# Second expert stage: two more leading weight places used once; the table of slots and the gate row fetched by ScalarE's queue

## What is computed

```python
tokens = modulate(x, norm_ffn[l], sh2, sc2)            # layer 0: context and latent, 512 tokens; layer 1: latent, 256
f = hier_moe(tokens, w_group[l], b_group[l], w_expert[l], b_expert[l], w1[l], w3[l], w2[l])
x = x + gt2 * f                                        # gt2: the gate row, 1024 numbers, one row for all tokens
```

## Time and profile before

| | |
|---|---|
| median of 3 runs | 2339.06 us (2337.82 to 2340.0) |
| the profiled execution | 2338.98 us |
| its span in the trace | 2337.2 us |
| busy: PE, DVE, ACT, POOL | 2186.6, 976.9, 347.4, 168.1 us |
| moved by DMA | 603.00 MB, mean 258 GB/s |
| granted clock of TensorE | 0.992 |
| stage 0, first to last `up` | begins at 367 us |
| stage 1, first `up` to last `add_pair` | 1112.6 to 1573.3 us |

### The profile page before, as it was taken

One profiled execution on the slowest core, in us unless ns is written; L12 is line 12 of the kernel. 1 busy time (PEld: TensorE's weight loads), 2 busy tenths in 40 slices (PEclk: granted clock), 3 DMA queues, 4 the chain that ended last, 5 costly groups with the idle time before them and its releaser, 6 DMA issues.

```text
span 2337.2 us, 25791 instructions
## 1 busy us (share of the span) xinstructions
PE 2186.6 (94%) x9558; PEld 1099.7 (47%) x9558; DVE 976.9 (42%) x1821; ACT 347.4 (15%) x943; POOL 168.1 (7%) x206
## 2 busy tenths in 40 slices
PE   5989999999999999989999888899899999999998
PEld 2436554333333344455333333335668744567843
DVE  3567433444433357573222222234721345561245
ACT  2006211000000010061000000001520001341100
POOL 1210002000000002230100000000000000000000
PEclk9999999999999999999999999999999999999999
DMA  9674557999999952244999999994324444514442
GB/s 374 248 278 154 198 181 302 420 420 421 422 421 421 421 224 72 75 169 162 364 420 420 420 421 421 421 382 126 109 72 158 153 167 134 180 37 136 152 145 98
DMA packets 150764, 603.00 MB, mean 258 GB/s; under 512 B 12660, under 2 KB 25716, under 8 KB 101136
## 3 DMA queue, kind: packets, MB, share of 16 engines
q1 hardware_dynamic: 145264, 595.26, 65.2%
q0 software_dynamic: 4736, 5.99, 0.7%
q10 hardware_dynamic: 672, 0.49, 0.1%
HBM read 606.89 MB, written 4.72 MB: 262 GB/s over the span
## 4 chain that ended last, share of the span: by engine, by line
PE 71%; DMA 12%; DVE 11%; ACT 2%; POOL 2%; issue 2%; SPq 1%; DVEq 0%; ACTq 0%; POOLq 0%
PE psum L2810 15%; DMA extra<-in_w 11%; PE psum L3024 10%; PE psum L3046 8%; PE psum L2327 7%; PE psum L2851 7%; PE psum L2820 6%; PE psum L2241 4%; PE psum L2905 4%; PE psum L2469 2%; PE psum L2340 2%; POOL rstd L500 1%; PE psum L2549 1%; DVE arena L1840 1%; PE psum L2588 1%
## 5 line engine op out<-in xcount | busy, mean ns | idle before, releaser
L1753 DVE TENSOR_TENSOR X<-X,psum 128x512 f32<-128x512 f32 x192 | 132.1, 688 | 269.4 <-PE psum L2820 268.4
L2810 PE MATMUL psum<-ring,arena 128*64 128x512 f32 x608 | 220.7, 594 | 12.6 <-DMA ring<-in_w 12.6
L3024 PE MATMUL psum<-hT,ring 128*128 128x256 f32 x1024 | 222.9, 381 | 2.6 <-DVE hT L1872 2.6
L2810 PE MATMUL psum<-arena 128*64 128x512 f32 x512 | 221.9, 595 | 0.7 <-ACT arena L968 0.7
L3024 PEld LDWEIGHTS psum<-hT,ring 128*128 128x128 f32 x1024 | 195.5, 191 | 29.7 <-DVE hT L1872 3.0
L2820 PE MATMUL psum<-arena 128*128 128x512 f32 x384 | 178.3, 601 | 0.0
L2327 PE MATMUL psum<-ring,hT 128*128 128x512 f32 x384 | 167.9, 593 | 1.9 <-DVE hT L1528 0.7
L2851 PE MATMUL psum<-ring,arena 128*64 128x512 f32 x408 | 167.3, 594 | 0.9 <-DVE arena L1844 0.9
L2241 PE MATMUL psum<-con,arena 128*128 128x128 f32 (+1 forms) x848 | 120.7, 282 | 33.0 <-DVE arena L1840 10.5
L2851 PE MATMUL psum<-extra,arena 128*64 128x512 f32 x328 | 146.4, 596 | 0.0
L2241 PEld LDWEIGHTS psum<-con,arena 128*128 128x128 f32 (+1 forms) x848 | 93.9, 142 | 88.2 <-issue 25.5
(11 more groups left out here) (396 smaller groups left out, 3073.8 us busy)
## 6 DMA issues: line engine op xcount, KB each, us to landing
ring<-in_w SPq DMA_DIRECT2D x127, 1024.0 KB, 21.9
arena<-in_w SPq DMA_DIRECT2D x72, 1024.0 KB, 18.8
ring<-in_w_ff SPq DMA_DIRECT2D x64, 1024.0 KB, 5.8
extra<-in_w SPq DMA_DIRECT2D x62, 1024.0 KB, 20.0
rows<-in_w SPq DMA_DIRECT2D x61, 1024.0 KB, 19.7
ring<-in_w_mod SPq DMA_DIRECT2D x32, 1024.0 KB, 13.5
gate<-in_w SPq DMA_DIRECT2D x29, 1024.0 KB, 23.0
hT<-in_w SPq DMA_DIRECT2D x18, 1024.0 KB, 16.5
```

The costliest lines, as they stand in the source:

```text
L1753: dve.tensor_tensor(x, x, bank, ALU.add).then_inc(v_free, 1)
L2810: inst = pe.matmul(out[64 * e:64 * e + 64, :], xgT[:, b, k, 64 * e:64 * e + 64], m, start=k == 0, stop=k == KB - 1)
L3024: inst = pe.matmul(bank[:, SEQ * f:SEQ * f + SEQ], w[k][:, at:at + P], hT[:, k, 0:SEQ], start=k == 0, stop=k == KB - 1)
```

## The change

1. Stage 1 has two more leading places, 9 (all of it) and 22 (new: `arena` 12288 to 14336). They are second and third in the order of use, so 20 chunks lead. They are used once; after them the old 18 places go round. SP issues place 9 behind place 7 and place 22 behind place 15, both with the same waits as these.
2. `pick_first`, `pick_second` and the scratch of the squares in stage 1 move to `arena` 8192 to 10240.
3. In both stages ACT, not SP, waits for `x_scattered` and fetches the table; it does so ahead of its first silu. SP goes from the leading chunks straight to the next chunk.
4. The gate row of stage 1 is fetched by ACT, when the first four chunks are used, ahead of the first silu. DVE's wait for it moves behind `slot_shares` of pair 0, ahead of line 1851.

```diff
-STEADY_PLACES = [[LEAD_PLACES[n][i % len(LEAD_PLACES[n])] for i in range(12 * LEAD_PAIRS[n])][-12:] for n in range(2)]
+ONCE = [9, 22]
+LEAD_ISSUE = [LEAD_PLACES[0], [12, 20, 21, 4, 5, 7, 9, 14, 17, 19, 18, 15, 22, 0, 6, 1, 2, 3, 8, 16]]
+LEAD_PLACES[1][1:1] = ONCE
+def lead_sequence(n):
+    places = list(LEAD_PLACES[n])
+    again = [p for p in places if p not in ONCE]
+    while len(places) < 12 * LEAD_PAIRS[n]:
+        places += again
+    return places[:12 * LEAD_PAIRS[n]]
+LEAD_SEQUENCE = [lead_sequence(n) for n in range(2)]
+STEADY_PLACES = [x[-12:] for x in LEAD_SEQUENCE]
...
-        pick_first = arena[:, 13312:13824].rearrange("p (t n) -> p t n", t=4)
+        pick_first = arena[:, 9216:9728].rearrange("p (t n) -> p t n", t=4)
...
-        pick_second = arena[:, 12800:13312].rearrange("p (t n) -> p t n", t=4)
+        pick_second = arena[:, 9728:10240].rearrange("p (t n) -> p t n", t=4)
...
-            at = {15: 10240, 16: 15360, 17: 6144, 18: 2048, 19: 4096}[i]
+            at = {15: 10240, 16: 15360, 17: 6144, 18: 2048, 19: 4096, 22: 12288}[i]
...
-                    squares([2, 3], arena[:, 12288:14336].rearrange("p (t n) -> p t n", t=2))
+                    squares([2, 3], arena[:, 8192:10240].rearrange("p (t n) -> p t n", t=2))
...
-                def pair(b, more=True):
+                def pair(b, more=True, first=False):
+                    if first:
+                        act.wait_ge(x_scattered, 16 * (8, 12)[l])
+                        act.dma_start(slot_tab, slot_table[l][0:EXPERTS * SLOTS].rearrange("(p e) w -> p e w", e=PAIRS)).then_inc(table_in, 16)
                     act.wait_ge(used, chunks.next(4))
+                    if first and l:
+                        act.dma_start(gate[:, 1, 0:1], gate_rows[1:2, 1, 0:1].to_broadcast([P, 1, D])).then_inc(gate_in[1], 16)
                     act.activation(siluG, psum[:, 4, :], ACT.Silu).then_inc(sil_ready, 1)
...
-                pair(0)
+                pair(0, first=True)
...
                     slot_shares(n)
+                    if not adds:
+                        dve.wait_ge(gate_in[1], 16 + 16 * l)
                     gates = gate_of(n)
...
                 slot_rows()
-                dve.wait_ge(gate_in[1], 16 + 16 * l)
                 pair(0, adds=False)
...
-                for n, place in enumerate(LEAD_PLACES[l]):
+                for place in LEAD_ISSUE[l]:
+                    n = LEAD_PLACES[l].index(place)
+                    if before[place] is not None:
+                        freed.n = before[place] + 1
+                        sp.wait_ge(used, freed.value())
...
                         if place == 7:
                             sp.wait_ge(value_made, 14)
-                            gate_load(gate[:, 1, 0:1], 1, 1, 1)
+                        if place == 22:
+                            sp.wait_ge(c_pv, len(C_STEPS))
...
-                    chunk(n // 12, n % 12)
-                sp.wait_ge(x_scattered, 16 * (8, 12)[l])
-                sp.dma_start(slot_tab, slot_table[l][0:EXPERTS * SLOTS].rearrange("(p e) w -> p e w", e=PAIRS)).then_inc(table_in, 16)
+                    first_chunk(n, place)
                 for n in range(len(LEAD_PLACES[l]), 12 * LEAD_PAIRS[l]):
                     chunk(n // 12, n % 12)
```

More of the change, by code:

```diff
@@ L340, in slot_at @@
                 return hT[:, 4:8, :].rearrange("p a n -> p (a n)")
-            if i >= 20:
+            if i in (20, 21):
                 return extra[:, i - 20, :]
-            at = {15: 10240, 16: 15360, 17: 6144, 18: 2048, 19: 4096}[i]
+            at = {15: 10240, 16: 15360, 17: 6144, 18: 2048, 19: 4096, 22: 12288}[i]
             return arena[:, at:at + CHUNK]
@@ L349, in build @@
         zeroed = sem("zeroed")
-        loaded = [sem(f"loaded{i}") for i in range(22)]
+        loaded = [sem(f"loaded{i}") for i in range(23)]
         used = sem("used")
@@ L2871, in moe @@
                 tallies.update({chunk_in[i]: 2 for i in STEADY_PLACES[l]})
-                slots.places, slots.at = LEAD_PLACES[l], 0
+                slots.places, slots.at = LEAD_SEQUENCE[l], 0
                 for n in range(LEAD_PAIRS[l]):
@@ L3146, in experts, with part, chunk, first_chunk @@
             def experts(l):
-                def chunk(pair, j):
+                def part(pair, j):
                     expert = bass.ds(2 * pair + j % 2, 1)
                     if j < 8:
-                        load(rows_of(t["w1" if j < 4 else "w3"][l, expert], KB, 4 * (j // 2 % 2), 4))
-                    else:
-                        load(rows_of(t["w2"][l, expert], 4, 2 * ((j - 8) // 2), 2))
+                        return rows_of(t["w1" if j < 4 else "w3"][l, expert], KB, 4 * (j // 2 % 2), 4)
+                    return rows_of(t["w2"][l, expert], 4, 2 * ((j - 8) // 2), 2)
+                def chunk(pair, j):
+                    load(part(pair, j))
+                def first_chunk(n, place):
+                    src = part(n // 12, n % 12)
+                    k = src.shape[1]
+                    dst = slot_at(place)[:, 0:k * src.shape[2]].rearrange("p (k n) -> p k n", k=k)
+                    sp.dma_start(dst, src).then_inc(loaded[place], 16)
                 nt = 4 - 2 * l
-                slots.places, slots.at = LEAD_PLACES[l], 0
+                slots.places, slots.at = LEAD_SEQUENCE[l], 0
+                before = {place: slots.user.get(place) for place in LEAD_PLACES[l]}
+                assert [slots.take()[0] for _ in LEAD_PLACES[l]] == LEAD_PLACES[l]
                 def store_rows():
```

## The result

The changed kernel took 2344.65 us in the median of 7 runs (2341.29 to 2348.37), the kernel before 2339.06 beside it (7 runs, 2335.72 to 2340.19): ratio 1.0022, 95% interval 1.0012 to 1.0032. It is slower by 0.2%, where 4.3 us less were forecast. The profiled execution took 2344.65 us, its span 2342.8, which is 5.6 more than before.

What follows compares the result with a forecast made beforehand. Stage 1 was taken to end when the weight stream has moved its bytes, stage 0 to be paced by PE. 2338.98 - 5.8 (stage 1) + 1.5 (stage 0) = 2334.7 us; own range 2333.8 to 2336, wider range 2332.3 to 2338.4.

Steps and rivals of the forecast that it cites:

- (a) to (c): Stage 1: two more leading chunks, gate row moved into the full stream, SP restarting without the scatter wait; gain 5.8 us together.
- two chunks less the gate row: Stage 1 stream: two more leading chunks save 5.1 us, and the gate row costs 1.3 of it.
- the gate row in it: Stage 1: the gate row enters the full stream as half a chunk, costing 1.3 us, from 0 to about 2.
- restart: Start of stage 1: SP, not waiting for scatters, issues chunk 20 at 1116.1; 2.0 us of the 5.8 gain.
- I take 1.5 us lost, bounds 0 and 4: Stage 0, pair 0: gather and table land later beside SP's earlier stream; both waits run side by side, the larger counts.
- The table's term: Stage 0: table fetched by ACT after a 3.7 us scatter lands in 5.5 us, making line 1840 1.4 us late.
- The gather's term: Stage 0: pair 1's gather lands in 8.0 us instead of 4.5, delaying the activation's turn by 0.7 to 1.5 us.
- Rival (3): Stage 0: the table stands behind SP's chunks, some 15 us, line 1840 10.9 us late, total 2344.1; chance 0.04.
- (d): Start of stage 1: table there at 1127, gate row with 14.8 us for a 5.9 us landing; waits covered by PE's 36 us.
- SP's chunks at 3.7 us after the first `up`: Sign for both stages: SP issues chunks at 370.6 and 1116.1, 3.5 us after 367.07 and 1112.60, no table in its queue.
- the pace of 26.5 and 30.5 us: Sign in stage 1: the silus' pace still goes from 26.5 to 30.5 us, but a pair later or less.
- no wait of PE for weights in stage 0: Sign in stage 0: the forecast would be wrong if PE waited for weights there.

Runs made afterwards that it cites:

- the second run: The changed kernel run once more, unaltered, against the kernel before: 2345.63 against 2340.26 us, ratio 1.0016.

## Why the prediction was wrong

**Stage 1, (a) to (c): right in kind, 5.8 forecast, 4.0 measured.** The 4.0 (3.6 in the second run) lies near the lower bound given, 3.8. Its terms: two chunks less the gate row, 3.8 forecast (5.1 - 1.3), 2.9 measured; the gate row in it 1.3 forecast, 2.0 measured, at the upper bound given; restart 2.0 forecast (5.8 - 5.1 + 1.3), 1.5 measured with the table in time (the denser restart of the kernel without added places gave 2.4).

**Stage 0: the step that failed**, "I take 1.5 us lost, bounds 0 and 4". It was 8.7: 5.2 for the table and 3.5 for the clock, with the gather underneath.

- *The table's term, 1.4.* It was 5.2 (3.4 from the scatter and 3.4 from the table, less the 1.7 of slack, make 5.1 of it). The scatter took 5.5 us where I took 3.7 from a scatter beside one leading chunk, though the view of all twelve had 4.9. The table took 7.3 where I took 5.5, "nearer to the short end". My upper bound of 8.0 held for the table, but stood on the short scatter. The nearest row for a small transfer beside a full stream was the gather's 8.0, and 7.3 is close to it, with a quarter of the bytes per row: here bytes were the wrong measure of nearness.
- *No term for the clock.* A PE that waits 5.5 us in two pieces was costed as lateness alone. The 3.5 us behind it (0.5 and 3.0) are work at half clock, shown by the kernels that kept PE busy. The trace before has several stretches where the clock dips (0.66 from 345 to 355 us and again from 1095 to 1105), so it could have been asked. The Trainium skill (TensorE: Matmul & The Clock Gate, "What's actually happening") says that an idle TensorE falls back to 1.2 GHz; the trace agrees, with 0.50 from 386 to 395 us, around a wait of 3.5 us. The forecast should have carried it as a possible cost of every wait that it put on PE.
- *The gather's term* was right in kind and about 1 us short: 9.0 us to landing where I took 8.0 and at most 8.8, and the rows' turn 2.1 us late where I had 1.1. It lay under the table's lateness, as forecast.

**Rival (3)**, the one on the other side, gave 2344.1, near the measured 2344.65, but by a mechanism that did not happen: that it came close is luck. The table did not stand behind SP's chunks (7.3 us, not 15). The 3.4 us that it took longer are under half of the loss; the scatter and the clock made the rest. The rule of the Trainium skill that I cited (DMA: Bandwidth & Descriptors, "Queues, rings and completion order") was not contradicted by this. What I read into it, that waiting for neighbours only would be cheap, was wrong: beside the stream the table took 3.8 us more than without it (7.3 against 3.5).

**"All of it is under PE's cover" (d)** held in the first trace of the changed kernel only because the table came just in time; in the second pair 0 was 1.0 us late. PE's cover does not cover everything: with nineteen leading chunks and pair 0 of stage 1 5 us late, stage 1 took 434.1, where the restart (2.4) and one chunk (2.55) should have given 431.6. About 2.5 us were lost, as the stream waits for PE's releases at its start. With the restart alone and the same lateness no such loss shows.

**What held:** SP's chunks at 3.7 us after the first `up` in both stages (3.5 forecast); the pace of 26.5 and 30.5 us in stage 1; no wait of PE for weights in stage 0; nothing lost in the moved picks and scratch, as stage 0 is whole once its table is back on SP, with picks and scratch still moved.

**What stays open:** how the 7 us of a 128 KB transfer beside the stream are made up, which no view here resolves, why the gate row costs 2.0 us for half a chunk's bytes, why the table of the same stage 1 takes 3.8 us in one execution and 6.4 in another, and when a short wait of PE costs clock: in stage 1, waits of 0.8 and 1.4 us ahead of the activation's turn were followed by a `w2` product of 8.8 and 8.7 us, waits of 1.2 and 1.5 by one of 7.09.

## To carry to other kernels

The place in a queue can act as a priority: the small transfer that others waited for took 3.9 us ahead of the bulk in the bulk's own queue and 6.9 to 7.3 on a free queue beside the bulk. Before an early restart of a stream, list every small transfer in flight at that moment (scatters, gathers, tables) and cost each at the slowest landing that the trace shows beside a full stream. Where a wait falls on TensorE, allow for the product behind it at half clock: 3.5 us here for waits of 2.0 and 3.5, 1.7 us for a single wait of 1.9 (the kernel in which SP waits for the scatters). And compare stages over several traces: the same stage 1 gave 431.6 to 433.5 us.

## What was not expected of the hardware

- On ACT's queue the table of 128 KB took 3.5 us with no stream, 3.8 to 6.4 beside the sparse restart of the changed stage 1, and 6.9 to 7.3 beside two or more chunks; ahead of the stream in SP's queue it took 3.9 in stage 0. The last scatter took 2.1 us without the stream and 5.5 to 6.9 beside it in stage 0.
- Around and after PE's wait of 3.5 us the granted clock was 0.50 for 9 us, 6.4 of them with PE at work, and one product of 7.09 us took 10.11. With 2 and 4 idle matmuls in these waits it stayed at 1.00.
